# A transformer trunk on one core: cutting two feed-forward stages into other parts, and giving the modulation sums a buffer of their own

## The chip, the cores and the metric

The kernel runs on one core of one Trainium2 chip. The time is that of the device for one execution, in microseconds (us); the table below has the median of three runs and one further execution that was profiled.

## What is computed

Two layers (`DEPTH` 2) over 512 latent tokens and 256 context tokens of width 1024, in float32. Cut to what matters here:

```
mod_l = silu(c) @ ada_w[i] + ada_b[i]          # 9 x 1024 shifts, scales, gates; mod_c the same from c_ctx
def ffn_half_step(xs, md, k, g, w_in, w_out):
    h = modulate(rms_norm(xs, g), md[3*k], md[3*k+1])
    gate, up = split(h @ w_in)                 # w_in 1024 x (2 x 2816)
    return xs + 0.5 * md[3*k+2] * ((silu(gate) * up) @ w_out)      # w_out 2816 x 1024
layer 0: FFN 0 -> multi-scale pooling -> FFN 1
layer 1: FFN 2 -> differential attention -> FFN 3 (latent tokens only)
```

FFNs 0, 1 and 2 work on all 768 tokens, FFN 3 on 512.

## The kernel before, in words

**Data.** Activations lie transposed: a chunk is 128 features on the partitions by 768 tokens. A row of weights `w` is used as a high and a low part (`w_hi`, `w_lo`, fp32r), as are the activations (`h_hi`, `h_lo`), and a product is three matmuls: hi by hi, hi by lo, lo by hi. ScalarE (ACT) writes `w_hi` (`split_hi`, L966), VectorE (DVE) writes `w_lo` (`split_lo`, L2203), and the DMA queue of SyncE (SP) brings `w_raw` (`load_unit`, L666), which waits until the split of the unit before in that buffer is done. There are two weight buffers, `ch` 0 and 1.

**Pairs and parts.** D_FF is 22 chunks (`FC`). An in-pair is the gate and the up chunk of one of the 22: two units (`unit`, L1642; `chunk`, L1534) of 8 K-steps, each K-step 3 products by 2 token segments (512 and 256 wide), so 96 matmuls. ACT takes the silu, DVE multiplies (`prod`, L2442), ACT writes `a_hi`, DVE writes `a_lo` (L2449). When a part of `kp` chunks is ready, four out-pairs follow (`OUT_PAIRS`): eight units of `kp` K-steps, each of which makes one chunk of the FFN's output summed over the part's chunks. DVE adds it to the stream `xT` with the gate (`add_out`, L2452; two instructions, L2456). FFNs 0 and 3 have two parts of 11 (`FP`). The last out-pair of FFN 0 is `tail_pe` (L1551): the 512-wide segments of both units first, then the sums of squares of the next norm (`sums_most` L1806, `sums_last` L1812), which wait for POOL's running sum `sqa` (L826), then the 256-wide segments and `spread` (L1820), which waits for POOL's power (L882). DVE's side of that tail is `pool_dve` (L2628), called from L2882; ahead of it DVE computes scales, gates and the bands of the pooling (L2862 to L2881).

**The block stage** (FFNs 1 and 2, `block_pe` L1725, `block_dve` L2385, `block_act` L1217). Here a gate/up pair is made by a 2 by 2 block scheme of seven products (P1, P6, P2, P5, P7, P3, P4) instead of eight, each of 12 matmuls 384 wide, so 84 per pair. ACT and DVE combine and split weight quarters of 512 columns for it (`block_t` L2238, `block_w_hi` L1143, `block_w_lo` L2262); SP loads the quarters (`quarters`, L676) once both splits of the last out-pair are done. `BLK_PARTS` (L58) holds per part: first chunk, chunks, how many of them are made whole (before the scheme's sums are ready, in `b_hi`), and the first block pair's number. FFN 1 has 11 whole chunks with their four out-pairs and then the block stage with parts of 6 (3 whole, 3 by blocks) and 5; FFN 2 is all block stage. When a part's out-pairs end, `block_ahead_lo` (L2273) makes the first products' weights of the next part, between the last two `add_out`.

**Granules.** Beside the pairs of FFNs 0, 1 and 3 the modulation `silu(c) @ ada_w` is computed in granules of 384 columns (`ADA_CH` 3). `beside` (L97) says which pair has one: FFN 0 has 26 of them (pairs 1 to 26), FFN 1 has 15, FFN 3 has 2. A granule is loaded (`load_granule`, L658) in two halves of 768 KB; DVE sums it over K with 16 instructions in two halves (`half_granule`, L2218), all of them into `ada_acc`. The first of them waits until the granule before has been taken out of `ada_acc` in full. ACT and POOL take it out in three bf16 parts: ACT `first_part` (L971), POOL subtracts (L891), ACT `other_parts` (L978), POOL, ACT. PE sums the parts over the partitions (`reduce_granule`, L1654, 18 small matmuls) one pair later. In an out-pair DVE has both halves ahead of `add_out` (L2499), and ACT has `first_part` between the two `split_hi` (L1124).

The order of the work is written out by hand, per engine, with a table of spans (`spans`, L112); each engine runs its list in order and waits on semaphores. The loops that the change touches:

```python
56: BLKS = (1, 2)
58: BLK_PARTS = {1: ((11, 6, 3, 0), (17, 5, 0, 3)),
85: ADA_L1 = (7, 15, 0, 2)
2224:                     if j == 0:
2225:                         dve.wait_ge(part_ready, PARTS3 * c + 1)
2500:                 if ada:
2501:                     half_granule(k, q * PART_PAIRS + FP + m - 1, 0)
2502:                     half_granule(k, q * PART_PAIRS + FP + m - 1, 1)
```

## Time and profile before

| | |
|---|---|
| median of 3 runs | 2485.64 us (2482.87 to 2485.89) |
| the profiled execution | 2487.29 us |
| its span, first to last instruction | 2485.5 us |
| PE (TensorE matmul) busy | 2441.7 us, 98% of the span |
| DVE / ACT / POOL busy | 1650.7 / 917.2 / 432.7 us |
| granted TensorE clock, mean | 0.997 of full |
| FFN 0 with its granules (from the trace) | about 64 to 612 us |
| pooling | about 612 to 680 us |
| FFN 1: whole part / block stage | about 680 to 992 / 992 to 1212 us |

Busy time of PE counts overlapping matmuls once; a matmul's end is modelled, so what a matmul costs is read from start to start. In rows of the timeline, times are from the span's start; "idle before" stands in square brackets with what released the engine.

### The profile page before, as it was taken

To read this page: it belongs to the slowest core of one execution; us is meant where nothing else is said; L and a number is where in the kernel's file an instruction comes from. 1 tells how busy PE (TensorE), PEld (TensorE's weight loads), DVE (VectorE), ACT (ScalarE), POOL (GpSimd) and SP (SyncE) were. 2 spreads that over 40 slices of the span, in tenths; PEclk is the share of its full clock that TensorE was granted. 3 is DMA by queue.
4 is the path that set the end of the run, shared out by engine and by line. 5 is a ranking of instruction groups with operands and counts; after the bars stand their busy time and mean duration, and the time that the engine had idled before them with its cause. 6 is when DMAs were issued, how large, how long until landed. Compare 5 with 4: busy or idle time off the path is not lost.

```text
span 2485.5 us, 40998 instructions
## 1 busy us (share of the span) xinstructions
PE 2441.7 (98%) x14665; PEld 2180.0 (88%) x14665; DVE 1650.7 (66%) x2612; ACT 917.2 (37%) x1457; POOL 432.7 (17%) x530
## 2 busy tenths in 40 slices
PE   8999999999899999999999999999999999999999
PEld 7888888888888888999889999999889988888887
DVE  6888678873888867847684757575877775643332
ACT  4333223331733313424442423243555564331221
POOL 0112121212211211000200000001567762000000
PEclk9999999999999999999999999999999999999999
DMA  7546445541154542222222222123110112433332
GB/s 235 167 139 169 131 127 146 158 121 41 35 169 139 169 131 68 77 68 64 62 63 68 76 59 77 51 85 93 27 52 25 51 34 68 128 100 95 93 108 87
DMA packets 367471, 239.51 MB, mean 96 GB/s; under 512 B 8114, under 2 KB 366099, under 8 KB 367379
## 3 DMA queue, kind: packets, MB, share of 16 engines
q1 hardware_dynamic: 366928, 238.12, 33.2%
q8 instruction: 55, 0.90, 0.2%
q14 instruction: 38, 0.30, 0.0%
q10 hardware_dynamic: 450, 0.18, 0.0%
HBM read 236.18 MB, written 2.10 MB: 96 GB/s over the span
## 4 chain that ended last, share of the span: by engine, by line
PE 75%; issue 13%; DVE 5%; POOL 3%; ACT 2%; DMA 1%; SPq 0%; POOLq 0%; ACTq 0%; DVEq 0%
PE pu L1539 46%; PE pu L1741 15%; PE pv L1931 5%; PE pu L1949 1%; POOL ada_acc L891 1%; PE pu L1968 1%; DVE xn L2556 1%; DVE h_lo L2563 1%; PE pv L1959 1%; PE pu L1581 1%; PE pu L1611 1%; PE pv L1662 1%; POOL rr L926 0%; PE pv L1581 0%; DVE w_lo L2205 0%
## 5 line engine op out<-in xcount | busy, mean ns | idle before, releaser
L1539 PE MATMUL pu<-h_hi,w_hi 128*128 128x512 f32 x1520 | 437.6, 351 | 1.7 <-DVE w_lo L2205 1.0
L1539 PE MATMUL pu<-h_lo,w_hi 128*128 128x512 f32 x1520 | 436.3, 350 | 0.0
L1539 PE MATMUL pu<-h_hi,w_lo 128*128 128x512 f32 x1520 | 436.0, 350 | 0.0
L2205 DVE TENSOR_TENSOR w_lo<-w_raw,w_hi 128x1024 fp32r<-128x1024 f32 (+3 forms) x206 | 275.3, 1338 | 178.0 <-ACT w_hi L969 172.5
L969 ACT ACTIVATE w_hi<-w_raw 128x1024 fp32r<-128x1024 f32 (+3 forms) x206 | 218.8, 1063 | 432.1 <-PE pu L1539 399.5
L2232 DVE SCALAR_TENSOR_TENSOR ada_acc<-ada_raw,cs,ada_acc 128x384 f32<-128x384 f32 x602 | 345.2, 615 | 11.2 <-DVE ada_acc L2232 2.0
L891 POOL TENSOR_TENSOR ada_acc<-ada_acc,ada_parts 128x768 f32<-128x768 f32 x86 | 147.4, 1714 | 773.7 <-ACT ada_parts L976 718.9
L1539 PEld LDWEIGHTS pu<-h_hi,w_hi 128*128 128x128 f32 x1520 | 243.9, 188 | 43.0 <-DVE w_lo L2205 1.4
L1539 PEld LDWEIGHTS pu<-h_hi,w_lo 128*128 128x128 f32 x1520 | 245.0, 188 | 39.8
L1539 PEld LDWEIGHTS pu<-h_lo,w_hi 128*128 128x128 f32 x1520 | 243.6, 188 | 38.7
L2456 DVE SCALAR_TENSOR_TENSOR xT<-pu,gate,xT 128x512 f32 (+3 forms) x140 | 82.8, 628 | 284.2 <-PE pu L1539 281.0
L1539 PE MATMUL pu<-a_hi,w_hi 128*128 128x512 f32 (+1 forms) x660 | 193.8, 353 | 0.7
L1539 PE MATMUL pu<-a_hi,w_lo 128*128 128x512 f32 (+1 forms) x660 | 194.0, 353 | 0.0
L1539 PE MATMUL pu<-a_lo,w_hi 128*128 128x512 f32 (+1 forms) x660 | 192.7, 351 | 0.0
L976 ACT ACTIVATE ada_parts<-ada_acc 128x768 bf16<-128x768 f32 x43 | 36.3, 845 | 321.7 <-PE pv L1662 308.6
L1741 PE MATMUL pu<-s_part,w_hi 128*128 128x384 f32 x540 | 145.9, 334 | 0.2 <-DVE xT L2456 0.2
L826 POOL TENSOR_TENSOR sqa<-sq 128x768 f32<-128x768 f32 (+2 forms) x6 | 8.8, 1475 | 698.5 <-ACT sq L1014 689.4
L1539 PEld LDWEIGHTS pu<-a_hi,w_hi 128*128 128x128 f32 x660 | 107.4, 188 | 18.8 <-issue 0.4
L1153 ACT ACTIVATE w_hi<-w_raw 128x512 fp32r<-128x512 f32 x135 | 83.7, 624 | 105.8 <-DVE w_raw L2254 77.1
L1539 PEld LDWEIGHTS pu<-a_hi,w_lo 128*128 128x128 f32 x660 | 107.1, 188 | 17.4
L1539 PEld LDWEIGHTS pu<-a_lo,w_hi 128*128 128x128 f32 x660 | 106.7, 188 | 17.8
L1539 PE MATMUL pu<-b_lo,w_hi 128*128 128x512 f32 x448 | 114.2, 336 | 0.0
(329 smaller groups left out, 5010.1 us busy)
## 6 DMA issues: line engine op xcount, KB each, us to landing
ada_raw<-in_ada_w SPq DMA_DIRECT2D x86, 768.0 KB, 4.7
w_raw<-in_ffn_w_in SPq DMA_DIRECT2D x116, 512.0 KB, 3.9
w_raw<-in_ffn_w_out SPq DMA_DIRECT2D x40, 704.0 KB, 4.5
w_raw<-in_ffn_w_in SPq DMA_DIRECT2D x108, 256.0 KB, 3.1
w_raw<-in_diff_w_qkv SPq DMA_DIRECT2D x21, 512.0 KB, 5.2
w_raw<-in_ffn_w_out SPq DMA_DIRECT2D x24, 384.0 KB, 3.3
first_raw<-in_ada_w SPq DMA_DIRECT2D x8, 1024.0 KB, 11.0
w_raw<-in_ffn_w_out SPq DMA_DIRECT2D x24, 320.0 KB, 3.3
```

The source lines that it names most:

```text
L891: nc.gpsimd.tensor_tensor(rest, rest, ada_parts[:, i, :], ALU.subtract).then_inc(rest_ready, 1)
L969: act.activation(w_hi[:, ch, 0:k * P], w_raw[:, ch, 0:k * P], ACT.Copy).then_inc(hi_ready[ch], 1)
L976: act.activation(ada_parts[:, 0, :], ada_acc[:].rearrange("p s n -> p (s n)"), ACT.Copy).then_inc(part_ready, 1)
L1153: act.activation(w_slot(w_hi, wx_hi, p), w_source[p], ACT.Copy).then_inc(blk_hi, 1)
L1539: last = pe.matmul(banks(ch, s_), w[:, j, :], r[:, SEG[s_]], start=(j == 0 and i == 0), stop=(j == k - 1 and i == 2))
L1581: last = pe.matmul(wide_bank(i, c, s_), w[:, j, :], x_[:, j, seg(i, s_)], start=(j == 0 and n == 0), stop=(j == k - 1 and n == 2))
L1611: last = pe.matmul(tail_bank(i, ch, s_), w[ch][:, j, :], x_[:, j, seg(i, s_)], start=(j == 0 and n == 0), stop=(j == DC - 1 and n == 2))
L1741: last = pe.matmul(pu[:, bank_of[p], 0:HN], w_[:, j, :], x_[:, j, :], start=(not adds and j == 0 and i == 0), stop=(j == HK - 1 and i == 2 ...
L1931: last = pe.matmul(pv[:, t % 2, at:3 * DV], x_[:, j, t * P:(t + 1) * P], aw[w_][:, j, at:], start=(j == 0 and i == 0), stop=(j == DC - 1 a ...
L2205: dve.tensor_tensor(w_lo[:, ch, 0:k * P], w_raw[:, ch, 0:k * P], w_hi[:, ch, 0:k * P].bitcast(F32), ALU.subtract).then_inc(split_ready[ch], 1)
L2232: last = dve.scalar_tensor_tensor(ada_acc[:, s_, :], ada_raw[:, b, i, :], w, ada_acc[:, s_, :], ALU.mult, ALU.add)
L2456: last = dve.scalar_tensor_tensor(xT[:, m, SEG[s]], banks(ch, s), gate[:, gk, s, m], xT[:, m, SEG[s]], ALU.mult, ALU.add)
```

## The change

- FFN 0 is cut in three parts of 8, 8 and 6 chunks instead of two of 11: 34 pairs instead of 30.
- FFN 1 has 8 whole chunks with their four out-pairs instead of 11; the block stage has 14 chunks in three parts of 6 (3 whole), 3 and 5. So 11 chunks are made by blocks instead of 8.
- 29 granules stand beside FFN 0 instead of 26, and 12 beside FFN 1 instead of 15.
- A granule's sum runs in a new buffer `ada_run`, laid over the part of `a_lo` that a part of 8 leaves free; only the last step writes `ada_acc`, and the wait for the granule before moves from the first step to the last (not in FFN 3).
- In an out-pair with a granule DVE does one half of it ahead of each `add_out`; ACT does `first_part` behind both `split_hi`.
- FFN 2's tables have other block numbers, with the same parts; FFN 3 is as it was.

```diff
-FFN_PAIRS = PARTS * PART_PAIRS
+FFN_PARTS = {0: ((0, 8), (8, 8), (16, 6)), 1: ((0, 8),), 3: ((0, FP), (FP, FP))}
+FFN_PAIRS = {k: sum(kp + OUT_PAIRS for _, kp in parts) for k, parts in FFN_PARTS.items()}
...
-BLK_PARTS = {1: ((11, 6, 3, 0), (17, 5, 0, 3)),
-             2: ((0, 6, 3, 8), (6, 6, 0, 11), (12, 5, 0, 17), (17, 5, 0, 22))}
-BLK_AT = {1: PART_PAIRS, 2: 0}
+BLK_PARTS = {1: ((8, 6, 3, 0), (14, 3, 0, 3), (17, 5, 0, 6)),
+             2: ((0, 6, 3, 11), (6, 6, 0, 14), (12, 5, 0, 20), (17, 5, 0, 25))}
+BLK_AT = {1: FFN_PAIRS[1], 2: 0}
...
+GATE_COUNT = FFN_PARTS[0][0][1] - 2
-ADA_L1 = (7, 15, 0, 2)
+ADA_L1 = (10, 12, 0, 2)
...
+def parts_of(k):
+
+    return [(q, f0, kp, f0 + OUT_PAIRS * q, k not in BLKS and f0 + kp == FC) for q, (f0, kp) in enumerate(FFN_PARTS[k])]
...
+        run_skip = sb("run_skip", [P, (FP + FFN_PARTS[1][0][1]) * NT], F32, running)
+        ada_run = sb("ada_run", [P, 2, ADA_COLS], F32, running)
...
                         if ada[1]:
                             other_parts(k, p - SUM_LAG)
-                        for ch in range(2):
-                            if nxt_:
+                        if nxt_:
+                            for ch in range(2):
                                 split_hi(ch, PAIR_FFN[k] + p + 1, nxt_)
-                            if ada[0] and ch == 0:
-                                first_part(k, p - 1)
+                        if ada[0]:
+                            first_part(k, p - 1)
...
-                k, x_hi, x_lo = FP, a_hi, a_lo
+                k, x_hi, x_lo = FFN_PARTS[0][-1][1], a_hi, a_lo
...
+                run = ada_acc if k == 3 else ada_run
...
-                    if j == 0:
+                    if j == (0 if k == 3 else DC - 1):
                         dve.wait_ge(part_ready, PARTS3 * c + 1)
...
-                            last = dve.tensor_scalar(ada_acc[:, s_, :], ada_raw[:, b, i, :], w, None, ALU.mult)
+                            last = dve.tensor_scalar(run[:, s_, :], ada_raw[:, b, i, :], w, None, ALU.mult)
...
-                            last = dve.scalar_tensor_tensor(ada_acc[:, s_, :], ada_raw[:, b, i, :], w, ada_acc[:, s_, :],
-                                                            ALU.mult, ALU.add)
+                            last = dve.scalar_tensor_tensor((ada_acc if j == DC - 1 else run)[:, s_, :], ada_raw[:, b, i, :], w,
+                                                            run[:, s_, :], ALU.mult, ALU.add)
...
-                if ada:
-                    half_granule(k, q * PART_PAIRS + FP + m - 1, 0)
-                    half_granule(k, q * PART_PAIRS + FP + m - 1, 1)
                 for ch in range(2):
-                    add_out(ch, b + FP + m, chunks[ch], gk, n)
+                    if ada:
+                        half_granule(k, p0 + kp + m - 1, ch)
+                    add_out(ch, b + kp + m, chunks[ch], gk, n)
                     if nxt:
-                        split_lo(ch, b + FP + m + 1, nxt)
+                        split_lo(ch, b + kp + m + 1, nxt)
```

The rest of the diff puts the part's first chunk, size and first pair (`f0`, `kp`, `p0`) in the place of `q * FP`, `FP` and `q * PART_PAIRS` on every engine, and `GATE_COUNT` in the place of `FP - 2`.

## Rows read from the trace of the kernel before

**Rows 1.** Windows: us, busy us of the engines, PEclk, DMA share, GB/s
```profile
63.80:596.80 533.00, 532.55 (x3409) 463.06 (x3410) 402.73 (x570) 161.96 (x202) 96.75 (x61) 1.00 0.48 138
684.80:992.20 307.40, 306.45 (x1952) 264.55 (x1950) 237.18 (x335) 93.10 (x116) 51.23 (x30) 1.00 0.47 136
```

**Rows 2.** The chain of waits: start, us, what; stretches of PE
```profile
168.41 16.91 PE pu L1539 x96
...
385.17 17.19 PE pu L1539 x96
...
1054.58 49.92 PE pu L1539 x288
1104.50 72.80 PE pu L1741 x420
```

**Rows 3.** The chain in FFN 1: POOL's first subtraction of two neighbouring granules
```profile
720.36 1.67 POOL ada_acc L891
...
738.05 1.66 POOL ada_acc L891
```

**Rows 4.** Windows: one in-pair of FFN 0 with its granule
```profile
185.40:202.73 17.33, 17.33 (x121) 15.18 (x118) 15.13 (x21) 6.04 (x8) 3.32 (x2) 1.00 0.53 151
```

**Rows 5.** From in-pairs to out-pairs in FFN 0: PE's chain, DVE's timeline
```profile
237.74 23.00 PE pu L1539 x132
...
241.83 2.41 DVE L2449 TENSOR_TENSOR a_lo<-prod,a_hi 128x768 fp32r<-128x768 f32 x1
```

**Rows 6.** End of FFN 0, DVE's timeline: first small operation, first addition of the tail
```profile
599.91 0.28 DVE L2656 TENSOR_TENSOR mod<-pv,par 128x30 f32<-128x30 f32 x2
...
609.78 0.74 DVE L2516 SCALAR_TENSOR_TENSOR xT<-pu,gate,xT 128x512 f32<-128x512 f32 x1
```

**Rows 7.** End of FFN 0: PE's chain and timeline, POOL's timeline
```profile
589.78 7.08 PE pu L1539 x40
...
611.45 0.39 PE L1547 MATMUL pu<-a_hi,w_lo 128*128 128x512 f32 x1
612.58 0.38 PE L1810 MATMUL pv<-ones,sqa 128*128 128x1 f32 x2 [0.75 <-POOL sqa L826]
...
613.64 1.55 PE pu L1547 x12
...
618.43 1.05 PE L1825 MATMUL pv<-ident,rms 128*128 128x128 f32 x8
...
624.41 0.36 PE L2083 MATMUL pu<-w_hi,h_hi 128*128 128x256 f32 x1 [0.98 <-DVE h_lo L2563]
...
611.26 1.27 POOL L826 TENSOR_TENSOR sqa<-sqa,sq 128x512 f32<-128x512 f32 x1 [7.57 <-ACT sq L1025]
616.45 1.02 POOL L882 TENSOR_TENSOR rms<-var,nhalf 128x4 f32<-128x4 f32 x1 [3.92 <-DVE var L2546]
```

**Rows 8.** Windows: two neighbouring stretches of the attention, the second at the lower clock
```profile
1773.00:1777.00 4.00, 1.93 (x13) 1.14 (x11) 2.59 (x7) 1.34 (x3) 2.83 (x7) 1.00 0.01 2
1777.00:1784.00 7.00, 6.07 (x24) 5.50 (x24) 4.59 (x12) 5.58 (x12) 0.94 (x2) 0.52 0.00 0
```

**Rows 9.** Block stage, from block pair to out-pairs of a part of 5: timeline
```profile
1177.14 0.51 PE L1539 MATMUL pu<-b_hi,w_hi 128*128 128x512 f32 x2
...
1179.89 0.56 DVE L2313 TENSOR_TENSOR b_lo<-prod,b_hi 128x384 fp32r<-128x384 f32 x1 [0.59 <-ACT b_hi L1172]
```

**Rows 10.** FFN 2, from out-pairs of a part of 5 to the next part: timelines
```profile
1612.40 1.14 DVE L2456 SCALAR_TENSOR_TENSOR xT<-pu,gate,xT 128x512 f32 x2 [3.33 <-PE pu L1539]
...
1619.33 0.68 DVE L2267 TENSOR_TENSOR w_lo<-w_raw,w_hi 128x512 fp32r<-128x512 f32 x1
...
1623.68 1.14 DVE L2456 SCALAR_TENSOR_TENSOR xT<-pu,gate,xT 128x512 f32<-128x512 f32 x2
...
1614.70 19.45 SPq L680 DMA_DIRECT2D w_raw<-in_ffn_w_in  x10
...
1624.87 0.45 PE L1741 MATMUL pu<-s_part,w_hi 128*128 128x384 f32 x1 [0.17 <-DVE xT L2456]
```

More of the change, by code:

```diff
@@ L728, in out_pair @@
                     if ada:
-                        load_granule(n, q * PART_PAIRS + FP + m - 1, ada)
-                for q in range(PARTS):
-                    if n in BLKS and q:
-                        load_block(n)
-                        break
+                        load_granule(n, p0 + kp + m - 1, ada)
+                for q, f0, kp, p0, last in parts_of(n):
                     if q == 0 and ADA_COUNT[n]:
                         for f in range(int(n in (0, 1, 3)), 2):
-                            in_pair(0, f, False)
+                            in_pair(f0, p0, f, False)
@@ L1140, in ffn_act @@
                     else:
-                        out_pair(OUT_PAIRS - 1, nxt if last else DC, [beside(k, p0 + PART_PAIRS - 1, lag) for lag in (1, SUM_LAG)])
+                        out_pair(OUT_PAIRS - 1, nxt if last else DC, [beside(k, p0 + kp + OUT_PAIRS - 1, lag) for lag in (1, SUM_LAG)])
+                if k in BLKS:
+                    block_act(k)
             def block_w_hi(g, p, free=None):
@@ L1679, in ffn_pe @@
                 n = FFN_N[k]
-                for q in range(PARTS):
-                    if k in BLKS and q:
-                        block_pe(k)
-                        break
-                    b = PAIR_FFN[k] + q * PART_PAIRS
+                for q, f0, kp, p0, ends in parts_of(k):
+                    b = PAIR_FFN[k] + p0
                     first = 0
@@ L1692, in ffn_pe @@
                         first = 1
-                    for lo, hi, ada in spans(k, q * PART_PAIRS, first, FP, SUM_LAG):
+                    for lo, hi, ada in spans(k, p0, first, kp, SUM_LAG):
                         with pe.Fori(lo, hi) as f:
@@ L1704, in out_pair @@
                                 amid()
[L1705 to L1706 removed]
+                            unit(ch, b + kp + m, kp, lambda j: a_hi[:, j], lambda j: a_lo[:, j], n,
+                                 acts=k * FC + f0 + kp)
                         if wait_mod:
@@ L1709, in out_pair @@
                         if ada:
-                            reduce_granule(k, q * PART_PAIRS + FP + m - SUM_LAG, ada)
+                            reduce_granule(k, p0 + kp + m - SUM_LAG, ada)
                     first = k == 0 and q == 0
                     if first:
-                        out_pair(0, beside(k, FP, SUM_LAG), 1)
-                    final = k == 3 and q == PARTS - 1
-                    for lo, hi, ada in spans(k, q * PART_PAIRS + FP, int(first), OUT_PAIRS - int(q == PARTS - 1), SUM_LAG):
+                        out_pair(0, beside(k, kp, SUM_LAG), 1)
+                    final = k == 3 and ends
+                    for lo, hi, ada in spans(k, p0 + kp, int(first), OUT_PAIRS - int(ends), SUM_LAG):
                         with pe.Fori(lo, hi) as m:
                             out_pair(m, ada)
-                    if q == PARTS - 1 and k < 3:
+                    if ends and k < 3:
                         tail_pe(FFN_NORM[k])
@@ L2461, in ffn_dve @@
                 n, gk = FFN_N[k], 2 * (k % 2)
-                for q in range(PARTS):
-                    if k in BLKS and q:
-                        block_dve(k)
-                        break
-                    b = PAIR_FFN[k] + q * PART_PAIRS
-                    a_ = k * FC + q * FP
-                    for lo, hi, ada in spans(k, q * PART_PAIRS, 0, FP - 1):
+                for q, f0, kp, p0, last in parts_of(k):
+                    b = PAIR_FFN[k] + p0
+                    a_ = k * FC + f0
+                    for lo, hi, ada in spans(k, p0, 0, kp - 1):
                         if k == 3 and q == 0 and lo in HALF_AT:
```

89 lines of the change are left out of this document (44 added, 45 removed).

## The prediction, made blind

> **What bounds the kernel now.** I read the windows by stage first. From the first full pair of FFN 0 to its last whole out-pair PE is busy 532.55 of 533.00 us, and in the whole part of FFN 1 306.45 of 307.40 us, at full clock; DVE is busy for about three quarters of both [rows 1]. So in these stages a time is a count of matmuls times their spacing, and an edit that only frees DVE, ACT or POOL buys nothing: at most the 0.45 and 0.95 us in which PE isn't busy. Next the chain of waits, for that spacing. An in-pair of 96 matmuls comes as 16.91 us in some places and as 17.19 us in others, with nothing waited for [rows 2]: matmuls run in one of two rhythms (about 0.174 and 0.177 us each). FFN 0 has both, 11 in-pairs with a granule in the fast one and 8 in the slow one. In FFN 1 the granules follow at 17.69 us [rows 3], so all of its whole pairs are slow. The block stage has one rhythm: five block pairs, 420 matmuls, in 72.80 us, 14.56 us a pair, and the out-pairs of its part of 6 at 0.1733 us a matmul [rows 2]. Last I looked for the places where PE does wait: the end of FFN 0 and the handovers of the block stage, below.
>
> **The change, part by part. Gains.** Three chunks of FFN 1 move from whole pairs to block pairs. A slow pair is 17.19 us less the part that its modelled end overlaps the next one, 17.1 us; 3 x (17.1 - 14.56) = 7.6 us saved. Out-pairs keep their matmuls (22 K-steps per output chunk), but the 3 K-steps of 8 chunks that move to a block part, 144 matmuls, run at 0.1733 instead of about 0.1775: 0.6 us saved. The three granules that move to FFN 0 take their 18 small matmuls with them: nothing in sum.
>
> **The own buffer and the new order** save nothing by themselves, as PE didn't wait for them; what they do is keep the shorter out-pairs safe. An in-pair costs DVE 15.13 of 17.33 us [rows 4]. An out-pair of 8 chunks has the same 96 matmuls; on DVE it has two additions of 1.14 us [rows 10] in the place of the product (about 1 us) and of `a_lo` (2.41 us [rows 5]), so some 14 us. ACT's and POOL's taking-out of the granule before ends some 6 us into the pair, when DVE would want `ada_acc` from about 2.5 us on; with the wait at the last step nobody stands. On SP the next load of buffer 0 is now queued behind the second half granule (done at about 16 us of the pair), lands some 4 to 5 us later, and is wanted 8.5 us into the next pair. The 16 further out units of both FFNs together bring 32 additions and as many smaller loads and splits, all beside PE work. If DVE came over 17.3 us a pair, this cover would be gone.
>
> **Entry to the out-pairs in FFN 0.** PE needs the last `a_lo` at the last K-step of the first unit. It ends at 244.24, 6.5 us after PE begins at 237.74 [rows 5]. With 11 K-steps PE wants it after 10.5 us, with 8 after 7.4, with 6 after 5.3; the smaller splits ahead of it make it earlier, to about 5.5 us. Cost 0.25 us (0 to 1).
>
> **End of FFN 0.** This is where the sum is decided. Let U be the end of the last whole out-pair, 589.78 + 7.08 = 596.86 [rows 7]. PE then has 66 matmuls 512 wide until 611.84. Meanwhile DVE does an addition, a split, and from 599.91 its list of small operations (scales, gates, bands), and comes to the tail's first addition only at 609.78 [rows 6]: 5.6 us after PE made it, hidden because PE was still in the second unit. From there POOL's sum starts 1.48 us later and `sums_most` at 612.58, 1.32 us after that [rows 7], U + 15.7. After the change the tail has 36 such matmuls, 8.2 us. DVE's list is unchanged, 9.87 us, and starts about U' + 2.1 (smaller split): first addition at U' + 12.0, `sums_most` at U' + 14.8. PE stands 6.6 us. Then 6 matmuls fewer stand before `sums_last` (12 take 1.55 us), so POOL's power ends 4.15 us after `sums_most` instead of 617.47 - 612.58 = 4.89, and `spread` needn't wait for PE as it does now (618.43): it starts at + 4.2. From `spread` to the first product of the pooling it is 5.98 us, a chain through DVE and ACT that stays. The pooling starts at U' + 25.0 instead of 624.41 - 596.86 = U + 27.55. But U' is later, as work left the tail: 60 matmuls moved ahead of it, 60 x 0.176 = 10.6 us. Cost: 10.6 + 25.0 - 27.55 = 8.05 us. In words: 30 narrow and 30 wide matmuls that covered DVE's list no longer do.
>
> **The clock in that stall.** In one place of the attention PE was busy for only 1.93 of 4 us, and the 7 us after that were granted 0.52 of the clock, nearly all at the lower level of 1.2 GHz [rows 8]. A stall of 6.6 us in one piece may do the same. What stands directly behind it on the path are `sums_most`, 6 matmuls and `sums_last`, 2.5 us at 2.4 GHz and twice that at 1.2: a cost of 0 to 2.5 us, I take 1.5, nearer to the row with the fall. The Trainium skill (TensorE: Matmul & The Clock Gate, "Why this matters for your kernels") says that idle time between bursts sends the clock back to 1.2 GHz; by it the term is the full 2.5 us.
>
> **Handovers of the new part of 3.** Into its out-pairs: the last `b_lo` ends at 1180.45, 3.3 us after PE starts the first unit at 1177.14 [rows 9]. A unit of 5 wants it after 4.2 us, one of 3 after 2.1: cost 1.3 us (1 to 1.5). Within them a unit is 3.12 us against 1.7 us of DVE, and a load is issued 4 us before it is wanted, where the 5-chunk load lands in 3.1: nothing (0 to 2). Out of them, by the row of FFN 2, whose part of 5 is just on the edge [rows 10]: the third pair's last addition begins at 1612.40, so that unit ended at 1612.2; SP issues the quarters 2.5 us later (1614.70); P1's weights are done 5.3 us after the issue (1619.33 + 0.68), P6 can start 10.2 us after it (1624.87), as it waits for the addition that stands behind six weight operations in DVE's list (1623.68). There the last unit ends only 10.4 us after 1612.2 (60 matmuls of 0.1733) and P1 ends 2.1 later, so all this is hidden but for the wait of 0.17 us that the row shows. With 3 chunks the last unit ends after 6.24 us and the issue is at + 2.25: P1 at + 7.6, 1.35 us late, ends at + 9.7; P6 at + 12.4, 2.75 us late. Cost 4.1 us (3 to 5; loads in a quieter stretch land up to 0.6 us sooner).
>
> **Sum.** FFN 0: 8.05 + 0.25 + 1.5 = + 9.8. FFN 1: - 7.6 - 0.6 + 1.3 + 4.1 = - 2.8. Together + 7.0 us. The profiled execution is 2487.29 us, with a span of 2485.5, and 1.65 above the median; I put the change on the median: 2485.6 + 7.0 = **2492.6 us**. About 0.2%, 5 us, is what a measurement of this kernel can tell from no change.
>
> **Rivals.** (a) The tail's stall doesn't come, in whole or most: DVE gets through its list before PE wants the sums. For it: the list already runs late without harm. Against: DVE would need 9.87 us of operations in some 3.5. Without the 8.05 and the 1.5: 2483.1 us, or near 2480 if the handover costs less too. Chance 0.14. (b) The rhythm turns: this is the one that ends not slower. Place: the 21 in-pairs and 12 out-pairs of FFN 0 and 11 pairs of FFN 1. All slow pairs fast would give about 2.4 (in-pairs, 8 x 0.3), 2.6 (out-pairs) and 3.7 us (11 x 0.34), 8.7 in all: 2484. It decides from about 23 pairs turned, when the 7.0 are gone; from 7 turned the change is within 0.2%. For it: the profile shows both rhythms with the same code. Against: nothing says which way, and all of FFN 0 slow would cost 4 us. Chance 0.2, typically 2487. (c) More stalls: the clock also falls in the handover of the part of 3, where PE stands 4.1 of 6 us. That is half of a stretch as in rows 8, 3.4 us, and the full 2.5 at the tail: 2497 us. The same section of the Trainium skill's TensorE: Matmul & The Clock Gate speaks for it. Chance 0.12. That the change doesn't do what it says I don't count: the counts of matmuls are fixed by the tables.
>
> **Chances.** The forecast has 0.54, with its own range 2488.5 to 2496.5: slower by over 5 us 0.40, same 0.14. (a): faster 0.08, same 0.06. (b): faster 0.03, same 0.15, slower 0.02. (c): slower 0.12. Together 0.11, 0.35, 0.54. The range leaves out the lowest of (a) and what is over (c): 2482.5 to 2498.
>
> **What would show it.** L1741 has 84 x 3 = 252 more matmuls at 0.1733, and L1539's with `h` 288 fewer. PE's largest new wait is L1810 on POOL `sqa`, some 6.5 us, with DVE L2516 straight behind L2625 and L2881, and PEclk under 1.00 there. In the block stage of FFN 1 PE L1741 waits twice for DVE (near 1.3 and 2.8 us), L1539 once for `b_lo` (1.3). FFN 0's out-pairs of 8 follow at 17.3 to 17.7 us without idle time; if they are longer, DVE has become the bound there and my cover is wrong. If PE waits little at L1810, (a) was right.

## The result and the profile after

The changed kernel takes 2496.41 us (median of 5, 2494.5 to 2501.15) where the kernel before takes 2485.64 beside it (2482.87 to 2487.49): a ratio of 1.0054 [1.0043, 1.0066], 13.4 us slower. The two medians themselves are 10.8 us apart, so a figure of the whole kernel below is good to some 3 us and no better. The forecast was + 7.0, with the sign right; put on the median of before, 2485.64, the ratio gives 2499, just over the upper end of the range (2498), while the median of 2496.41 lies inside it. The profiled execution of the changed kernel is 2496.41 us, with a span of 2494.3 and a mean clock of 0.995.

First its windows, the columns as in [rows 1]: FFN 0 to the end of the last whole out-pair; from there to the first product of the pooling; the pooling; FFN 1's whole part; its block stage.

```profile
62.00:608.76 546.76, 545.82 (x3528) 473.86 (x3527) 456.19 (x643) 172.65 (x221) 108.69 (x67) 1.00 0.49 144
608.76:637.78 29.02, 20.33 (x97) 18.38 (x96) 18.20 (x62) 8.44 (x12) 7.00 (x5) 0.76 0.08 24
637.78:698.60 60.82, 55.15 (x384) 50.50 (x385) 50.39 (x87) 42.27 (x79) 14.86 (x15) 0.97 0.14 35
698.60:1000.00 301.40, 299.27 (x1882) 265.45 (x1881) 252.16 (x355) 101.46 (x142) 42.40 (x24) 1.00 0.43 125
1000.00:1250.00 250.00, 244.74 (x1400) 227.97 (x1399) 160.18 (x281) 89.17 (x158) 14.36 (x11) 0.99 0.22 64
```

The first row answers to [rows 1]: PE is busy for all but 0.94 us, though DVE is now at 83%. The cover held, and nobody waits for the granules' buffers. The second row is where the time went: 29.02 us between the last whole out-pair and the pooling, PE busy for 20.33 of them, the granted clock 0.76. The kernel before needs 27.55 us there ([rows 7], 624.41 less 596.86), with 60 matmuls more to do. Now PE's waits of the changed kernel (us in total, times, the longest):

```profile
PE pv L1815 <- POOL sqa L835: 7.8, 4, 6.6
PE pu L1746 <- ACT p_held L1184: 2.6, 2, 1.5
PE pu L1746 <- DVE xT L2462: 2.4, 1, 2.4
```

Two of these are new: 6.6 us at `sums_most` (0.75 in [rows 7]), the 2.4 for `xT` in the block handover. The end of FFN 0 in detail, DVE's and POOL's timeline, and under it the chain (start, us, what), which answer to [rows 6, 7]:

```profile
608.95 1.14 DVE L2462 SCALAR_TENSOR_TENSOR xT<-pu,gate,xT 128x512 f32 x2 [4.20 <-PE pu L1545]
610.87 0.29 DVE L2659 TENSOR_TENSOR mod<-pv,par 128x39 f32<-128x39 f32 x2
...
620.73 1.40 DVE L2519 SCALAR_TENSOR_TENSOR xT<-pu,gate,xT 128x512 f32<-128x512 f32 x2
...
628.86 1.02 POOL L891 TENSOR_TENSOR rms<-var,nhalf 128x4 f32<-128x4 f32 x1 [5.38 <-DVE var L2549]
```

```profile
622.21 1.27 POOL sqa L835
623.52 1.87 PE pv L1815 x8
625.39 1.49 PE pu L1553 x6
626.88 1.50 PE pv L1821 x8
628.38 2.77 PE pu L1553 x12
631.15 1.72 PE pv L1830 x8
```

Read against the forecast, with U' = 608.76, the end of the last whole out-pair in the changed kernel: DVE's list takes 9.86 us as before and ends at 620.73, U' + 12.0 (forecast 12.0). `sums_most` starts at 623.52, U' + 14.8 (forecast 14.8). To there each number is as worked out. Then the matmuls take nearly twice as long: the 12 narrow ones ahead of `spread` 2.77 us where 12 took 1.55 in [rows 7]. POOL's power is done at 629.88, but PE comes to `spread` only at 630.95, because it is still in those 12. `spread` was forecast at U' + 19.0 and is at U' + 22.2; the pooling starts at U' + 29.0 instead of 25.0.

### The profile page after: what moved, and what is told of

Read it like the earlier page. It is cut to its first block, busy times and chain, and to the rows that moved or that the text cites. A ratio compares the mean times of both kernels' runs of the same rounds, so it can differ in the third digit from the quotient of the medians.

```text
span 2494.3 us, 41342 instructions
## 1 busy us (share of the span) xinstructions
PE 2439.2 (98%) x14629; PEld 2184.5 (88%) x14629; DVE 1708.1 (68%) x2705; ACT 930.3 (37%) x1497; POOL 436.5 (17%) x530
## 3 DMA queue, kind: packets, MB, share of 16 engines
q1 hardware_dynamic: 367280, 238.12, 32.9%
## 4 chain that ended last, share of the span: by engine, by line
PE 78%; issue 10%; DVE 6%; POOL 3%; ACT 2%; DMA 1%; SPq 0%; POOLq 0%; ACTq 0%; DVEq 0%
PE pu L1545 47%; PE pu L1746 17%; PE pv L1936 5%; PE pu L1954 1%; PE pu L1973 1%; POOL ada_acc L900 1%; DVE xn L2559 1%; PE pv L1964 1%; DVE h_lo L2566 1%; PE pu L1587 1%; PE pv L1843 1%; PE pu L1617 1%; PE pv L1668 1%; DVE w_lo L2210 0%; POOL rr L935 0%
## 5 line engine op out<-in xcount | busy, mean ns | idle before, releaser
L1545 PE MATMUL pu<-h_hi,w_hi 128*128 128x512 f32 (+1 forms) x1424 | 413.0, 352 | 1.6 <-DVE w_lo L2210 1.0
L1545 PE MATMUL pu<-h_lo,w_hi 128*128 128x512 f32 (+1 forms) x1424 | 411.8, 351 | 0.0
L1545 PE MATMUL pu<-h_hi,w_lo 128*128 128x512 f32 (+1 forms) x1424 | 410.3, 350 | 0.0
L978 ACT ACTIVATE w_hi<-w_raw 128x1024 fp32r<-128x1024 f32 (+4 forms) x216 | 215.9, 1000 | 504.4 <-PE pu L1545 463.6
L2210 DVE TENSOR_TENSOR w_lo<-w_raw,w_hi 128x1024 fp32r<-128x1024 f32 (+4 forms) x216 | 269.7, 1250 | 165.8 <-ACT w_hi L978 165.1
L2238 DVE SCALAR_TENSOR_TENSOR ada_run<-ada_raw,cs,ada_run 128x384 f32<-128x384 f32 x492 | 294.6, 640 | 7.3
L1545 PE MATMUL pu<-a_hi,w_hi 128*128 128x512 f32 x632 | 186.3, 353 | 0.9
L1545 PE MATMUL pu<-a_hi,w_lo 128*128 128x512 f32 x632 | 186.0, 353 | 0.0
L1545 PE MATMUL pu<-a_lo,w_hi 128*128 128x512 f32 x632 | 185.4, 352 | 0.0
L1545 PE MATMUL pu<-b_hi,w_lo 128*128 128x512 f32 x496 | 126.8, 336 | 0.0
```

The costliest lines, as they stand in the source:

```text
L978: act.activation(w_hi[:, ch, 0:k * P], w_raw[:, ch, 0:k * P], ACT.Copy).then_inc(hi_ready[ch], 1)
L1545: last = pe.matmul(banks(ch, s_), w[:, j, :], r[:, SEG[s_]], start=(j == 0 and i == 0), stop=(j == k - 1 and i == 2))
L2210: dve.tensor_tensor(w_lo[:, ch, 0:k * P], w_raw[:, ch, 0:k * P], w_hi[:, ch, 0:k * P].bitcast(F32), ALU.subtract).then_inc(split_ready[ch], 1)
L2238: last = dve.scalar_tensor_tensor((ada_acc if j == DC - 1 else run)[:, s_, :], ada_raw[:, b, i, :], w, run[:, s_, :], ALU.mult, ALU.add)
```

## The experiments

One table for all, as a reader can then compare. "Sums", "spread" and "pooling" are the starts of `sums_most`, of `spread` and of the first product of the pooling, in us after the end of the last whole out-pair, in the profiled execution. The medians of before beside the other kernels were 2482.7 to 2484.2 (the row shows one of them), so kernels are compared by their ratios. "Clock" is the mean granted clock over all runs of that kernel; 0.001 of it is 2.5 us of full clock.

| kernel | median us | ratio to before | clock | sums | spread | pooling |
|---|---|---|---|---|---|---|
| before | 2484.2 | | 0.997 | 15.7 | 21.6 | 27.6 |
| changed | 2496.4 | 1.0054 [1.0043, 1.0066] | 0.994 | 14.8 | 22.2 | 29.0 |
| e1_list_early | 2493.1 | 1.0039 [1.0025, 1.0053] | 0.994 | 12.6 | 20.0 | 26.8 |
| e2_block_as_before | 2497.1 | 1.0050 [1.0036, 1.0063] | 0.994 | 14.8 | 22.2 | 29.0 |
| e3_pe_kept_busy | 2494.3 | 1.0039 [1.0026, 1.0053] | 0.997 | 14.8 | 19.0 | 25.1 |
| e4_parts_868 | 2500.1 | 1.0065 [1.0051, 1.0078] | 0.995 | 15.0 | 23.3 | 30.2 |
| e5_add_first | 2495.7 | 1.0053 [1.0039, 1.0067] | 0.995 | 14.8 | 22.2 | 28.9 |
| e8_tail_first | 2490.1 | 1.0033 [1.0020, 1.0045] | 0.996 | 8.0 | 16.3 | 22.5 |
| e9_tail_and_add_first | 2491.8 | 1.0027 [1.0018, 1.0037] | 0.996 | 8.0 | 17.0 | 23.5 |
| e10_bands_split | 2492.3 | 1.0034 [1.0022, 1.0046] | 0.996 | 10.7 | 17.2 | 24.1 |
| e11_parts_778 | 2486.5 | 1.0010 [1.0001, 1.0019] | 0.996 | 11.0 | 17.3 | 23.7 |
| b1_before_tail_first | 2484.8 | 0.9998 [0.9989, 1.0007] | 0.997 | 14.8 | 20.6 | 26.5 |
| f1_before_list_longer | 2492.7 | 1.0043 [1.0029, 1.0056] | 0.995 | 22.3 | 32.9 | 39.0 |
| f2_778_block_before | 2486.6 | 1.0016 [1.0007, 1.0025] | 0.997 | 11.0 | 16.1 | 22.1 |
| f3_parts_778_alone | 2493.7 | 1.0040 [1.0026, 1.0054] | 0.995 | 15.0 | 22.9 | 28.9 |

**1. Is it the clock behind the stall?** 28 useless matmuls fill PE's wait, and nothing else moves:

```diff
+                if i == 1:
+                    for c in range(28):
+                        pe.matmul(pv[:, 3, 0:NL], wslot(w_hi, 0, k)[:, 0, :], x_hi[:, 0, SEG[0]], start=True, stop=True)
                 sums_most(i, 0)
```

> The edit: in the changed kernel, 28 more matmuls 512 wide, whose result nobody reads, stand in the tail of FFN 0 directly ahead of sums_most: 28 x 0.23 = 6.4 us, which fills PE's wait for DVE without moving it. Theory (about 4 us of the loss is the clock, which falls because PE stands idle for 6.6 us): sums_most begins at the same time after the last out-pair (14.8 us), the granted clock there stays 1.00, the matmuls between sums_most and spread take half as long, and the pooling starts at 25.0 instead of 29.0 us: about 2492.5 us, and the runs lie closer together. Rival (the clock is set by something other than PE's idle time, or spread waits for DVE or POOL anyhow): the time stays at 2496, with spread at 22 us after the last out-pair.

Windows of that kernel from the last out-pair to `sums_most`, and from there to the pooling, and under them the second one in the changed kernel:

```profile
607.27:622.07 14.80, 14.53 (x65) 11.67 (x64) 12.64 (x52) 3.58 (x5) 5.27 (x3) 1.00 0.11 37
622.07:632.37 10.30, 7.50 (x61) 7.13 (x61) 5.58 (x10) 4.87 (x7) 1.76 (x2) 1.00 0.15 44
```

```profile
623.52:637.78 14.26, 12.14 (x60) 11.96 (x61) 5.56 (x10) 4.87 (x7) 1.76 (x2) 0.62 0.04 11
```

The same work, 60 or 61 instructions of PE, takes 10.30 us at clock 1.00 and 14.26 at 0.62. 3.96 us were the clock alone, and they were had back in this stretch by making PE do more. In the whole kernel this is less sure: the median fell by only half of what was expected, and the ratio by 0.0015, 3.7 us, with intervals that overlap. The mean clock of its runs is 0.997, as in before. So of the forecast's terms the stall was right, and the clock was 4.0 where 1.5, at most 2.5, had been put down.

**2. The same stall in the kernel before.** The pair of small instructions for `edge_cols` is repeated, so that DVE's list is longer, with FFN 0 and 1 as they were:

```diff
-                for e_, at in ((0, 2 * HALO), (1, 2 * HALO + P - PAD)):
-                    last = dve.tensor_tensor(edge_cols[:, e_], ...
-                mod_link(last)
+                for _ in range(21):
+                    for e_, at in ((0, 2 * HALO), (1, 2 * HALO + P - PAD)):
+                        last = dve.tensor_tensor(edge_cols[:, e_], ...
+                    mod_link(last)
```

> The edit: in the kernel before, the pair of small DVE operations that makes edge_cols at the end of FFN 0 is done 21 times instead of once, each 0.32 us: DVE's list is 6.4 us longer and PE's wait at sums_most goes from 0.7 to 7.1 us, as long as in the changed kernel, with nothing else changed. Theory (a wait there costs its length and then the clock of the matmuls behind it, 4 us): the pooling starts 34.1 us after the last out-pair by the wait alone, 37 to 38 with the clock, against 27.7; the median is 9.5 to 10.5 us over before, with a mean clock of the runs near 0.995. Rival (the fall of the clock belongs to the changed kernel's shorter parts or to the run, not to the wait): 6.4 us over before and a clock of 0.997.

PE's wait, and the chain behind it (the longer list, 601.34 to 608.19, is 42 instructions in one row of DVE's timeline):

```profile
PE pv L1810 <- POOL sqa L826: 8.3, 4, 7.3
```

```profile
615.25 1.86 PE pv L1810 x8
617.12 2.77 PE pu L1547 x12
619.88 1.50 PE pv L1816 x8
621.38 4.69 PE pu L1547 x21
```

The same 12 matmuls as in [rows 7], in the old kernel, took 2.77 us instead of 1.55, once PE had stood 7.3 us. `sums_most` came 6.6 us later than before and the pooling 11.4 later, and the whole kernel is 0.43% slower, 10.7 us. The wait alone makes the fall; shorter parts aren't needed for it. By the Trainium skill (TensorE: Matmul & The Clock Gate, "Why this matters for your kernels") an idle gap between bursts of matmuls brings TensorE back to the lower clock; this pair of runs agrees with it.

**3. Uncovering it by moving the list.** The part of DVE's list that needs only the modulation goes ahead of the last whole out-pair (a function `late_mods`, called there):

```diff
+                        if k == 0 and last and lo:
+                            late_mods()
                         with dve.Fori(lo, hi) as m:
                             out_pair(k, p0, ...
...
-            mod_link(scales(0, (1, 2)))
-            mod_link(gates(0, (1, 2)))
...
```

> The edit: in the changed kernel, the part of DVE's list of small operations that only needs the modulation (bias additions, scales, gates, pooling factors, about 6 us of the 9.9 us) is moved ahead of the work of the last whole out-pair of FFN 0; the bands stay where they are. Theory (the time above before is made at the end of FFN 0, where the shorter tail no longer covers this list, and where the clock then falls): the list left after the last out-pair is about 4 us, the first tail addition comes about 6 us sooner, PE's wait at sums_most falls from 6.6 to about 1.3 us, the clock stays at 1.00, and the pooling starts about 9 us sooner (5.3 of wait and 4.0 of clock): 2487 us where the changed kernel has 2496. If only the wait counts and the clock falls anyhow: 2491. Rival (the time lies in the parts themselves: more units, more additions, smaller loads, or a turned rhythm of the matmuls): the wait goes, but the span stays within 2 us of 2496, because another wait takes its place.

A miss: `sums_most` came 2.1 us sooner, not 5.3, PE still waited 4.5 us, and the clock fell as before. The list that was left took far longer than its share. DVE's timeline there:

```profile
610.49 1.93 DVE L2641 TENSOR_TENSOR edge_cols<-win,edge_sb 128x32 f32<-128x32 f32 x2
612.46 1.95 DVE L2646 SCALAR_TENSOR_TENSOR band_ends<-win 128x136 f32<-128x136 f32 x1
...
614.53 0.29 DVE L2646 SCALAR_TENSOR_TENSOR band_ends<-win 128x136 f32<-128x136 f32 x1
...
610.28 3.97 POOL L835 TENSOR_TENSOR sqa<-sqa,sq 128x768 f32<-128x768 f32 x2 [5.63 <-ACT sq L1023]
```

An instruction that takes 0.29 us takes 1.95 while POOL adds 768 columns, and 0.29 again when POOL is done at 614.25. In the changed kernel the list meets POOL's additions too, at `amul` and `gate`, and the toll is part of its 9.86 us:

```profile
612.94 1.95 DVE L2667 TENSOR_SCALAR gate<-mod 128x8 f32<-128x8 f32 x4
610.52 4.13 POOL L835 TENSOR_TENSOR sqa<-sqa,sq 128x768 f32<-128x768 f32 x2 [4.89 <-ACT sq L1023]
```

The first of the four `gate` ends with POOL's additions, at 614.67; away from them one is 0.16 us. Moving the list away moved the toll onto the bands. The Trainium skill (GPSIMD Engine Reference, "1. Specifications") says that POOL's interfaces to SBUF are shared with DVE, and names DVE's instructions in a 2-port perf mode and those with two inputs from SBUF as the ones that contend. `edge_cols` and `band_ends` have two inputs and agree; `gate` has one, and no row shows in which mode it runs. So the next step put the bands where DVE waits for PE anyhow, between the tail's first and second addition:

```diff
-                for ch in range(2):
-                    tail_chunk(1, 0, ch)
+                tail_chunk(1, 0, 0)
+                make_bands()
+                tail_chunk(1, 0, 1)
```

> The edit: the changed kernel with DVE's modulation list ahead of the last whole out-pair of FFN 0, as in e1_list_early, and in addition the bands (about 4 us) between the tail's first and second addition in place of ahead of both. In e1_list_early the first addition came at 9.8 us after the last out-pair, still behind the bands, two of which took 1.9 us each beside POOL's two additions of 768 columns. Theory (PE's wait at sums_most and the clock's fall behind it are what the end of FFN 0 costs): PE makes the first tail unit at 4.3 us after the last out-pair, so sums_most can follow the 36 wide matmuls at once, near 8.3 us; sums_last may wait 1 us for the bands; the clock stays at 1.00 and the pooling starts at about 20.5 us after the last out-pair instead of 29.0: 8 us less, 2488 us. Rival (the time is in something the shorter parts bring all along FFN 0, not at its end): the span falls by no more than 4 us.

`sums_most` follows the 36 matmuls at once, at 8.0. But `sums_last` then waits for the second addition:

```profile
617.31 0.95 PE L1815 MATMUL pv<-ones,sqa 128*128 128x1 f32 x8
621.87 1.16 PE L1821 MATMUL pv<-ones,sq 128*128 128x1 f32 x8 [2.78 <-ACT sq L1034]
```

and behind those 2.8 us of idle the clock was down again (the next 12 matmuls take 2.77 us). The pooling starts at 22.5 (expected 20.5), 6.5 sooner than in the changed kernel; the ratio gives 5.2 us back. A last order, e9 (both edits, e8's and that of part 6 below) with the bands in halves, only moved the wait back to `sums_most`:

> The edit: e9_tail_and_add_first, with the bands in two halves: the first two of the four groups ahead of the tail's first addition, where DVE stood idle for 2.0 us, the other two between the first and the second. In e9 and e8 sums_most came at 8.2 us after the last out-pair, but sums_last waited 2.8 us for the square of the second addition behind the bands, and after that wait the clock fell again (12 matmuls in 2.7 us in place of 1.5). Theory (each wait of PE in the tail costs its length and about as much again by the clock behind it): the second addition comes at 8.5 us, sums_last at 10 to 10.5, the clock stays, spread starts at 13.5 to 14 and the pooling at 19.5 to 20 us after the last out-pair, against 23.6 in e9: 3.5 us less, a median of 2487 to 2488.5, a mean clock of the runs above 0.996. Rival (what is left of the loss is no longer in the tail): within 1 us of e9, 2490.5 or more.

It gained nothing over e9 (1.0034 against 1.0027): the first half met POOL's additions (`edge_cols` 1.87 us and one `band_ends` 1.96, as above), so PE waited 2.5 us there. Its median is the one that the rival named, but it doesn't speak for the rival, as the wait that the edit was to remove was still there. A wait of 2.5, one of 2.8, one of 4.5 and one of 6.6 us: the clock fell behind each.

**4. The same order in the kernel before.**

> The edit: in the kernel before, the same as e8_tail_first: DVE's modulation list ahead of the last whole out-pair of FFN 0 and the bands between the tail's first and second addition. Theory (in the kernel before, the 66 wide matmuls of the tail hide this list but for 0.7 us): at most 0.7 us is gained, so 2484 to 2486 us, no difference that can be measured. Rival (the list is a cost in its own right wherever it stands): 2480 or less.

Level with before, with 0.9 us gained at `sums_most`. A list that is covered costs nothing wherever it stands, as the forecast had it.

**5. The parts of FFN 0.** One line of the table of parts, `(0, 8), (8, 6), (14, 8)`:

> The edit: FFN 0's parts are 8, 6 and 8 chunks instead of 8, 8 and 6, with everything else as changed. Theory (what matters is how much of PE's work lies between the last whole out-pair and sums_most): the tail has 48 matmuls 512 wide in place of 36, 10.9 us instead of 8.2, so PE's wait at sums_most is 3.9 us instead of 6.6; the larger last split makes it some 0.3 us later. That saves 2.5 us, and, if the shorter stall lets the clock be, up to 4 more: 2490 to 2494 us. Rival (the order of the parts is neutral, since the same matmuls are done in all, and the pooling's start is set elsewhere): 2496 us.

The wait at `sums_most` shrank as expected, to 4.1 us, but the kernel is not faster: 1.0065 against 1.0054, with intervals that overlap. PE's waits show a new one in the four out-pairs of 6 that have a granule, and the timelines of PE, DVE and POOL why:

```profile
PE pu L1545 <- DVE w_lo L2210: 7.4, 8, 1.5
```

```profile
387.83 0.58 PE L1545 MATMUL pu<-a_hi,w_hi 128*128 128x512 f32 x2 [1.28 <-DVE w_lo L2210]
...
403.40 0.62 PE L1545 MATMUL pu<-a_hi,w_hi 128*128 128x512 f32 x2 [0.70 <-DVE w_lo L2210]
...
377.48 2.06 DVE L2210 TENSOR_TENSOR w_lo<-w_raw,w_hi 128x768 fp32r<-128x768 f32 x1
379.47 2.14 DVE L2236 TENSOR_SCALAR ada_run<-ada_raw,cs 128x384 f32<-128x384 f32 x2
...
377.08 1.65 POOL L900 TENSOR_TENSOR ada_acc<-ada_acc,ada_parts 128x768 f32<-128x768 f32 x1 [12.06 <-ACT ada_parts L985]
379.69 1.70 POOL L900 TENSOR_TENSOR ada_acc<-ada_acc,ada_parts 128x768 f32<-128x768 f32 x1 [0.96 <-ACT ada_parts L991]
```

From 387.83 to 403.40 is one out-pair, 15.6 us, where its 72 matmuls take 12.5. DVE needs those 15 to 16 us: its own list and POOL's toll on it (`w_lo` 2.06 us, where it is 0.95 with POOL at rest). Parts of 7, 7 and 8 have 14.7 us of matmuls per out-pair and a tail of 48 wide matmuls. With e10's order of the list:

> The edit: e10_bands_split with parts of 7, 7 and 8 chunks in FFN 0 instead of 8, 8 and 6. The parts of 8, 6 and 8 lost because an out-pair of 6 chunks with a granule takes DVE 13.5 to 14.6 us, where PE has 12.5 us of matmuls: four such pairs, with waits of up to 1.5 us at each unit. An out-pair of 7 chunks has 14.7 us of matmuls. Theory (DVE's time per out-pair is a floor at about 14.6 us, and the tail is good as long as its wide matmuls cover DVE's list): no wait for w_lo in the out-pairs of 7 over 0.5 us, 48 wide matmuls in the tail, sums_most directly behind them, and the clock at 1.00: 2485 to 2487.5 us, or 1 to 2 us less than e10. Rival (the DVE floor is nearer 15 us than 14.6, with the granule's additions in it): seven out-pairs lose 0.3 us or more each, and it is no faster than e10.

2486.5 us, 1.0010: against the changed kernel's 1.0054 some 11 us are taken back, and the intervals are far apart. It comes near the kernel before, and doesn't beat it. Both readings hold in part: there are five waits for `w_lo` in the out-pairs, 2.0 us together, the longest 0.6. The parts alone, without the order, are not enough:

> The edit: the changed kernel with parts of 7, 7 and 8 chunks in FFN 0, and nothing else; DVE's list stays in one piece ahead of the tail. Theory (the parts decide how much of the list is covered, the order of the list the rest): 48 wide matmuls, 10.9 us, before sums_most, which comes 15.2 us after the last out-pair as in the parts of 8, 6 and 8, so PE waits 4.1 us and the clock falls behind it; the pooling starts 30 us after the last out-pair, which ends at about 606 us: 3 us less than the changed kernel, 2493.5 us, and 5 us or more over e11. Rival (the parts alone were the whole difference of e11): 2486 to 2488.

1.0040; PE waits 4.1 us at `sums_most`, the clock falls, and the pooling starts at 28.9. The order alone, with parts of 8, 8 and 6, had 1.0034 (e10). Both halves are needed: matmuls that cover, and a list that is short when it counts. (e10 and e11 also have e5's edit of the handover, which f3 lacks; alone it made no difference that can be told, see 6.)

**6. What the block part of 3 is worth.** First FFN 1's tables put back, with the parts of FFN 0 as changed:

> The edit: FFN 1 is set back to what it was before the change (11 chunks whole, block parts of 6 and 5, 12 granules in it), while FFN 0 keeps its parts of 8, 8 and 6 and its 34 granules go on as changed. Theory: FFN 1's share of the change was a gain of about 2 to 4 us with the handover of its part of 3 and the clock's fall in it (8.2 us of cheaper block pairs and out units against 1.3 of entry, 4.1 of handover and about 1.7 of clock would be a gain of 1.1), so this kernel has no wait of PE for p_held or xT in FFN 1, still 6.6 us at sums_most, and takes 2497 to 2500 us. Rival (the handover of the part of 3 costs more than its block pairs save): 2494 or less.

1.0050 against 1.0054: no difference that can be told. Then the last addition of the handover put directly behind the weights of P1:

```diff
                 if ch == 0:
                     block_t(g, T1)
                     block_w_lo(g, P1)
+                    if amid:
+                        amid()
```

> The edit: in the changed kernel, where the out-pairs of FFN 1's block part of 3 hand over to the next block part, DVE does the second of the two last additions directly behind the weight operation of P1, and no longer behind all operations of T1, P1 and T2. Theory (P6 waits 2.5 us there for that addition, and the clock falls just behind the two waits): the wait of 2.4 us of PE for xT falls under 1 us, which saves 1.7 us, and up to 1.7 more if the clock then stays: 2493 to 2495 us where the changed kernel has 2496.4. Rival (the weights of the next pair are late anyhow, so the wait moves on to p_held or w_lo): no change in the span, within 1 us.

Both theories were half right. The handover in the changed kernel, windows and timeline, answering to [rows 9, 10]:

```profile
1108.81:1118.25 9.44, 5.76 (x25) 5.47 (x25) 8.01 (x14) 4.35 (x8) 0.00 (x0) 0.86 0.28 80
```

```profile
1085.23 0.61 PE L1545 MATMUL pu<-b_hi,w_hi 128*128 128x512 f32 x2 [1.12 <-DVE b_lo L2319]
...
1110.11 0.41 PE L1746 MATMUL pu<-h_hi,w_hi 128*128 128x384 f32 x1 [1.30 <-DVE w_lo L2273]
...
1113.62 1.14 DVE L2462 SCALAR_TENSOR_TENSOR xT<-pu,gate,xT 128x512 f32<-128x512 f32 x2
...
1114.81 0.62 PE L1746 MATMUL pu<-s_part,w_hi 128*128 128x384 f32 x2 [2.38 <-DVE xT L2462]
```

In e5 the wait of 2.4 us is gone, and PE's other waits in this line grew: for `p_held` from 2.6 us to 4.0, for `w_lo` from 1.3 to 2.1. From the chain of e5, the load of the next weights, ACT's work on them, and PE:

```profile
1116.12 3.07 DMA w_raw<-in_ffn_w_in
...
1121.46 0.39 ACT p_held L1184
1121.90 8.25 PE pu L1746 x46
```

The next weights are late by themselves, through their load and their splits, so the wait moved on, as the rival had it: 6.3 us in all became 6.1, and the ratio (1.0053) tells no difference. e9, which has this edit and e8's, bears that out:

> The edit: e8_tail_first and e5_add_first together. Theory: both stalls gone but for the entry to the part of 3 and the weights of P1: 2485 to 2487 us, level with the kernel before. Rival (the change loses elsewhere too): over 2490.

It is level with e8, and 6.7 us over before, as its rival has it (over 2490). But it doesn't show that the change loses elsewhere, as the clock's fall in the tail was still there. Last, the block part of 3 taken out of the best version:

> The edit: e11_parts_778 with FFN 1 as in the kernel before (11 chunks whole, block parts of 6 and 5); the last addition of the block handover is as changed. Theory (FFN 1's share of the change is a gain once its second handover is mended: e11 has 551.6 us from FFN 1's first unit to FFN 2's, e2_block_as_before had 552.6, and the kernel before 554.2 to 556.4 with three granules, 1.8 us, more in it): 1 to 2 us over e11, 2487.5 to 2488.5. Rival (the forecast's 2.8 us of gain plus the 1.4 us that the mended handover gives back): 4 us over e11, 2490 or more. Other rival (the block part of 3 is worth nothing): level with e11.

1.0016 against 1.0010: 1.5 us, as expected, but inside both intervals. From FFN 1's first unit to FFN 2's the profiles give 552.7 us with the old tables and 12 granules (e2 and f2, 552.64 and 552.73), 552.1 with the new ones (mean of seven, 550.8 to 553.6), 551.3 with the edit of the handover as well (mean of four). The spread within the changed tables has a cause that rows show. The 420 matmuls behind the handover, in the first and in the second profile of the changed kernel:

```profile
1110.11:1187.23 77.12, 74.74 (x420) 74.43 (x421) 57.41 (x97) 33.61 (x64) 0.00 (x0) 0.98 0.24 71
```

```profile
1112.03:1187.81 75.78, 73.41 (x420) 72.82 (x421) 57.18 (x97) 33.39 (x64) 0.00 (x0) 1.00 0.25 72
```

Before has 72.80 us for them [rows 2]. The clock fell there in three of the seven profiles with the handover as changed (the first of the changed kernel, e3 and f3, 77.1 us each); in the other four these matmuls take 75.6 to 75.8 us, and in the four with e5's edit 75.7. FFN 1 takes 553.1 us with that fall, 551.3 without it, and 551.3 with the edit. So the edit wins back no waiting; at most it spares the fall, and four profiles can't tell that from chance. The block part of 3 is worth 0.6 us in the mean, 1.3 where the clock holds, and not 2.8.

**7. How far one execution differs from another.**

> The changed kernel once more, for a second profile. The profiled executions of the two kernels are 9.1 us apart, the medians 10.8 and the ratio says 13.4. Theory (the rest is the clock, which falls for longer or shorter in the same places from run to run: the runs of the changed kernel have a mean granted clock of 0.994, those of before 0.997): a second profile shows the same waits to 0.2 us, and differs from the first in the length of the stretches at the lower clock and in the rhythm of the pairs of FFN 0 and 1 alone. Rival: a wait that the first profile did not have.

> The kernel before once more, for a second profile: its first one, 2487.29 us, was the slowest of its runs. Theory: a usual execution is 3 us shorter, in the rhythm of FFN 1's pairs (556.4 us from FFN 1's first unit to FFN 2's in the first profile, 554.4 in b1_before_tail_first, which has the same code there) and in the attention stage (789.6 us where other profiles have 787.4 to 791.6). Rival: the first profile's stages come again to 0.5 us each.

The span of the second profile of the changed kernel is 2495.7, that of before 2482.4: 13.3 us apart, as the ratio says, where the first two are 8.8 apart. The first unit after the pooling and that of FFN 2, for before and for the changed kernel:

```profile
683.34 0.51 PE L1539 MATMUL pu<-h_hi,w_hi 128*128 128x512 f32 x2
...
1237.53 0.51 PE L1539 MATMUL pu<-h_hi,w_hi 128*128 128x512 f32 x2
```

```profile
699.82 0.51 PE L1545 MATMUL pu<-h_hi,w_hi 128*128 128x512 f32 x2
...
1251.88 0.52 PE L1545 MATMUL pu<-h_hi,w_hi 128*128 128x512 f32 x2
```

FFN 1 is 554.2 us in the second profile of before, 556.4 in the first, though its waits of 0.6 and 1.5 us are 0.9 and 1.2 in the second, the same in sum. In the changed kernel the waits came again to 0.1 us (6.6, 1.5 and 2.4).

## Why the prediction was wrong

The stages, each as the mean over the profiles of kernels that have the same code there (how many stands behind the mean), in us. The 1.35 for the three granules is an estimate from [rows 2, 3, 4]: an in-pair takes 17.33 or 17.69 us with one, 16.91 or 17.19 without.

| stretch | forecast | measured |
|---|---|---|
| to the end of the last whole out-pair (60 matmuls and three granules, 1.35, moved there; entry) | + 12.2 | + 13.3 (608.6, nine profiles; 595.3, four) |
| from there to the pooling | - 2.55 + 1.5 | + 1.5 (29.0 against 27.6) |
| pooling | 0 | + 0.3 (61.1, thirteen; 60.8, four) |
| FFN 1 (the three granules leave it) | - 2.8 - 1.35 | - 2.8 (552.1, seven; 554.8, four) |
| FFN 2 to the end | 0 | - 0.5 (1243.7, thirteen; 1244.2, four) |
| sum | + 7.0 | + 11.8; by the ratio + 13.4 |

- **What bounds it, the cover of DVE, the buffer, the out-pairs of 8**: right. PE's idle time in FFN 0 is 0.94 us.
- **Entry to the out-pairs of FFN 0**: right within what can be seen; no wait stands out there.
- **The stall at the end of FFN 0**: right. Its three times (12.0, 14.8, and PE's 6.6 us) are those of the trace. Rival (a) is refuted.
- **"The clock in that stall" is the step that failed.** It took the fall for sure enough to price it at 1.5, and gave it a ceiling of 2.5 us by doubling what stands between `sums_most` and the end of `sums_last`. It went wrong in treating the 12 matmuls behind them as still hidden behind POOL's power, because at full clock they were. At half the clock they take 2.7 us, end after the power, and hold `spread`, which itself is at half speed: 3.2 us to there and 0.7 more to the pooling. e3 and f1 measure 4.0 and 4.9 us. It isn't the whole miss: with 4.0 in the place of 1.5 the forecast would have been + 9.5. Of the 4.8 us between forecast and measured sum in the table it is 2.5; FFN 1 is 1.4 and the way to the end of the out-pairs 1.1. What a slow engine makes longer must be laid out again along the chain; it can't be looked up in a sum made at the full clock.
- **The three granules**: the prediction put moving them at nothing in sum, and in sum nothing shows against it. FFN 1 without them is 552.7 us (e2 and f2) against 554.8 with them: 2.1 us for three, where 1.35 was put down above. The same 0.8 us more in FFN 0 is most of what is over 12.2 in the first row.
- **Handovers of the part of 3**: PE waits 1.1 us for `b_lo` at the entry (forecast 1.3), 1.3 for P1 (1.35) and 2.4 for P6 (2.75). Start to start they cost more: the 144 matmuls of the out-pairs take 28.0 to 28.5 us where 144 x 0.1733 is 24.96, and the 420 behind them 75.6 to 75.8 where 72.80 were before, together 6.1 us against 5.4. And in the first profile the clock fell behind them: 12 matmuls took 3.44 us instead of 2.08 and the next 12 2.42, which is 1.7 us, or 1.3 over the 420. That is rival (c)'s mechanism, which had a chance of 0.12 and a time of 2497. In the second profile the same two waits (1.2 and 2.4 us) are not followed by it: the 12 matmuls take 2.20 us.
- **The block part's gain**: FFN 1 as a whole gave 2.2 us less than forecast, against the same code with the old tables (552.1 for 552.7, with - 2.8 forecast). 0.7 are the handovers, 0.6 the clock's fall as the mean of seven profiles, three of which have it. What is left, 0.8, is the saving itself, an estimate of 7.4 us (552.7 - 551.3 + 6.1) where 8.2 were forecast. The rhythm can do as much: the same ten whole in-pairs of before, 960 matmuls, took 173.9 to 176.0 us in four profiles.
- **Rhythm**, rival (b): it didn't decide, but it is why single profiles mislead. The same code reaches the end of FFN 0's out-pairs at 592.8 to 596.7 in before and at 607.1 to 610.2 in the changed kernel.
- **The range**: its top took rival (c) with the clock at 2.5 in the tail. With 4.0 there, (c) gives 2498.5, near the ratio's 2499. But that is a meeting of numbers and doesn't confirm (c): the fall in the handover came in the first profile and not in the second, which is the slower of the two (2497.8 against 2496.41 us).

Open: what sets the rhythm; why the clock falls in one execution and not in another with the same waits; and 1.6 us of the 13.4, which the profiles don't hold. The mean clock of all runs is 0.994 against 0.997, some 8 us of full clock. In the first profile the tail alone has 6.9 of them, (1 - 0.90) x 14.76 us up to `sums_most` (where PE mostly stood, so that it cost nothing) and (1 - 0.62) x 14.26 behind it. How long the low stretches last in runs without a profile isn't seen.

## What to carry to other kernels

Shortening the last piece of a stage takes away what covers the other engines' once-only work at its end: look up what DVE, ACT and POOL do there, and price the uncovered part before counting the gain. Price a stall of PE as its length plus the chain behind it at half the clock, laid out anew; if it can't go, useless matmuls in it may be cheaper than the clock (in e3 3.96 us in the stretch itself). A part's out-pair must be no shorter than the slowest other engine's list for it, with the toll of POOL on DVE in it.

## What the runs showed of the hardware

- With the same small delays in the tail the clock fell in one execution and not in another: from the start of the matmul ahead of it, `sums_most` comes after 0.52 us and `sums_last` after 0.36 in both. Windows from `sums_most` to the pooling, of e11 and of f2, which are the same code there:

```profile
617.20:629.97 12.77, 10.49 (x73) 10.08 (x73) 7.25 (x16) 5.51 (x8) 1.86 (x3) 0.87 0.05 15
```

```profile
615.65:626.87 11.22, 8.94 (x73) 8.56 (x73) 7.23 (x16) 5.51 (x8) 1.84 (x3) 1.00 0.06 17
```

  1.55 us between them. Every wait of 2.5 to 7.3 us at `sums_most` or `sums_last` was followed by the fall. But it isn't a matter of length alone: ahead of the pooling PE waits 2.8 us in e1 and in e8, and the 24 matmuls behind it take 2.94 us in e1 and 4.38 in e8.
- A small DVE instruction that reads two inputs takes 1.95 us beside POOL's additions, and 0.29 without; a `gate`, which reads one, is held as well (four take 1.95 us, one alone 0.16). Two such meetings in e1 added 3.3 us to a list that took 7.9.
- Medians of this kernel before were 2482.7 to 2485.6 in different sessions; ratios beside each other are what can be compared.
